# Index scores of a hybrid decoder block as 64-row products among MLA's first products, with turned blocks of x in places of their own

## What is computed

```python
h = rmsnorm(x, g[NORM_PRE_MIX])
(q_lat, kv_lat, k_rope, ..., idx_q, idx_k, idx_w, ...) = split_cols(h @ w_in[l])
# MLA: 8 heads of 128+64, from latents
q = rmsnorm(q_lat, q_norm) @ w_uq          # latents 384 wide
kv = rmsnorm(kv_lat, kv_norm) @ w_ukv      # latents 256 wide
# DSA's index scores: 8 heads of 64, one key shared by all heads
score = einsum('bth,bths->bts', iw, relu(einsum('bthd,bsd->bths', iq, ik)))
score = where(s <= t, score, -inf);  _, idx = top_k(score, 128)
```

## Time and profile before

| | us |
|---|---|
| median of 3 runs | 1501.98 (1501.86 to 1502.58) |
| the profiled execution | 1502.69 |
| its span in the profile | 1500.9 |
| PE busy | 1462.5 (97%) |
| DVE busy | 684.4 (46%) |
| ACT busy | 569.8 (38%) |
| mean granted PE clock | 0.997 |

### The profile page before, as it was taken

How to read it: one execution, slowest core, us unless ns; L and a number is a source line. 1 busy time by engine, 2 the same in 40 slices (tenths; PEclk the granted TensorE clock), 3 DMA queues, 4 the chain that set the end, 5 groups by cost and what they waited for, 6 DMA issues and landing times.

```text
span 1500.9 us, 17329 instructions
## 1 busy us (share of the span) xinstructions
PE 1462.5 (97%) x7180; PEld 1178.6 (79%) x7180; DVE 684.4 (46%) x1186; ACT 569.8 (38%) x920; POOL 99.7 (7%) x74
## 2 busy tenths in 40 slices
PE   6999999999999999999999999999999999999998
PEld 5957777887877788876776788897778888888886
DVE  3566565764333355444554344483355332222334
ACT  4444543214333243445345423454344342223321
POOL 1000000022220001000000001000000220011100
PEclk9999999999999999999999999999999999999999
DMA  5211132232311334440210333254121323233321
GB/s 178 79 38 46 43 112 78 91 104 79 99 56 57 93 113 156 148 145 15 70 57 3 125 117 136 85 173 137 56 85 57 112 84 113 84 99 99 95 102 56
DMA packets 118270, 137.87 MB, mean 92 GB/s; under 512 B 7043, under 2 KB 98432, under 8 KB 118192
## 3 DMA queue, kind: packets, MB, share of 16 engines
q1 hardware_dynamic: 115200, 126.17, 26.6%
q0 software_dynamic: 2704, 10.00, 1.9%
q10 hardware_dynamic: 288, 0.59, 0.1%
HBM read 134.61 MB, written 2.14 MB: 91 GB/s over the span
## 4 chain that ended last, share of the span: by engine, by line
PE 94%; ACT 2%; DVE 2%; issue 1%; DMA 0%; SPq 0%; DVEq 0%; ACTq 0%
PE dense L660 25%; PE dense L662 25%; PE dense L661 25%; PE score L773 3%; PE turned L790 3%; PE score L790 3%; PE turned L773 2%; PE turned L783 1%; PE score L763 1%; PE score L783 1%; DVE probs L1893 1%; ACT probsT L1268 1%; PE score L1166 1%; PE score L1152 0%; PE turned L1152 0%
## 5 line engine op out<-in xcount | busy, mean ns | idle before, releaser
L1739 DVE TENSOR_TENSOR weight_low<-raw,weight_high 128x2048 fp32r<-128x2048 f32 (+2 forms) x96 | 201.2, 2102 | 375.0 <-ACT weight_high L1268 374.9
L660 PE MATMUL dense<-hidden_high,weight_high 128*128 128x512 f32 (+1 forms) x840 | 327.0, 389 | 4.0 <-ACT vN L1268 2.5
L662 PE MATMUL dense<-hidden_high,weight_low 128*128 128x512 f32 (+1 forms) x840 | 320.7, 382 | 0.0
L661 PE MATMUL dense<-hidden_low,weight_high 128*128 128x512 f32 (+1 forms) x840 | 320.2, 381 | 0.0
L1268 ACT ACTIVATE weight_high<-raw 128x2048 fp32r<-128x2048 f32 (+4 forms) x156 | 220.8, 1440 | 257.5 <-PE dense L662 255.0
L660 PEld LDWEIGHTS dense<-hidden_high,weight_high 128*128 128x128 f32 x840 | 158.0, 188 | 34.2 <-ACT vN L1268 2.9
L662 PEld LDWEIGHTS dense<-hidden_high,weight_low 128*128 128x128 f32 x840 | 157.9, 188 | 31.0
L661 PEld LDWEIGHTS dense<-hidden_low,weight_high 128*128 128x128 f32 x840 | 158.1, 188 | 29.7 <-issue 0.7
L1734 DVE TENSOR_TENSOR weight_low<-raw,weight_high 128x1024 fp32r<-128x1024 f32 x58 | 74.9, 1334 | 67.5 <-ACT weight_high L1268 67.5
L660 PE MATMUL dense<-weight_high,up_high 128*128 128x512 f32 x256 | 99.6, 389 | 0.0
L661 PE MATMUL dense<-weight_low,up_high 128*128 128x512 f32 x256 | 99.6, 389 | 0.0
(11 more groups left out here) (311 smaller groups left out, 2326.9 us busy)
## 6 DMA issues: line engine op xcount, KB each, us to landing
raw<-in_w_in SPq DMA_DIRECT2D x34, 1024.0 KB, 5.3
raw<-in_mlp_w SPq DMA_DIRECT2D x32, 1024.0 KB, 5.3
raw<-in_w_branch SPq DMA_DIRECT2D x12, 1024.0 KB, 5.1
raw<-in_nsa_cmp_w SPq DMA_DIRECT2D x8, 1024.0 KB, 5.3
raw<-in_cross_wkv SPq DMA_DIRECT2D x8, 1024.0 KB, 5.6
raw<-in_w_in SPq DMA_DIRECT2D x9, 512.0 KB, 5.1
bias_strips<-bias_scratch POOLq DMA_DIRECT2D x8, 512.0 KB, 4.1
raw<-in_w_out SPq DMA_DIRECT2D x4, 1024.0 KB, 5.1
```

The source lines that it names most:

```text
L660: pe.matmul(out_ap, ah, bh, start=first, stop=False)
L661: pe.matmul(out_ap, ah, bl, start=False, stop=False)
L662: return pe.matmul(out_ap, al, bh, start=False, stop=last)
L1739: ins = V.tensor_tensor(dst, src, hi.bitcast(F32), ALU.subtract)
```

## The change

- **Start.** SP issues slab 0 right behind x and the six small loads behind it. The turned blocks 0 to 3 of x go to `W`, `SS`, `G[1]` and again `W` (`XB`), so that the first three wait for nothing but their scaling. Block 3 is turned in the middle of `("lat", 0)`, behind its first block's products. The small tables are turned after `("lat", 0)`, into `SS`. ACT copies half of slab 0 between the blocks of x. DVE makes the first half of slab 0's low part, POOL only the second. DVE copies the tables after the low part of slab 2.
- **Index scores.** One key tile holds the key twice, in rows 0 to 63 and 64 to 127. A product takes 64 rows of query and key; `index_pair` issues two of them, one on each half of the rows, for two heads. The products go through four places (`INDEX`), and product n waits for ACT's taking of n-4. Three pairs stand around the third turn of the latents; two stand in `m1`, three in `m2`, two in `m3`, two in `m4` of round 0. PE waits for the last taking after `m4`. ACT's ReLUs and DVE's sums are cut into pieces among the other steps: DVE does 16, then the rotation and a slab's low part, then 8.

```diff
-ikT = [at(f"index_k{i}", [P, T], 120 + 2 * i) for i in range(2)]
+ikT = at("index_k", [P, T], 120)
...
-product("setup", "V")
-for i in range(4):
-  product(("x", i), "V")
-for i in range(3):
+XB = [W, SS, G[1], W]
+for i in range(NT - 1):
+  part(None)
+  ready_at["x", i] = events[0]
+part(None)
+ready_at["x", NT - 1] = events[0]
+product(("lat", 0), "A", slab_at["lat", 0])
+part(None)
+ready_at["setup"] = events[0]
+for i in range(1, 3):
...
+INDEX = [S[0], S[1], PT, OT]
+INDEX_FIRST = 6
...
+hidden_split = sem("hidden_split")
+setup_taken = sem("setup_taken")
...
+  def load(s):
+      if s >= 2:
+          sp.wait_ge(low_ready, split_at[s - 2])
+      for src, view in slabs[s]:
+          sp.dma_start(view(raw[s % 2]), src).then_inc(loaded[s % 2], 16)
+  load(0)
...
-  def load(s):
-      if s >= 2:
-          sp.wait_ge(low_ready, split_at[s - 2])
-      for src, view in slabs[s]:
-          sp.dma_start(view(raw[s % 2]), src).then_inc(loaded[s % 2], 16)
-  for s in range(2):
-      load(s)
+  load(1)
...
-  g = product_at["setup"]
...
+  def turn_x(t):
+      pe.wait_ge(x_scaled, t + 1)
+      if t == NT - 1:
+          pe.wait_ge(hidden_split, 1)
+      for k in range(KD):
+          mm = pe.transpose(XB[t][:, k // 4, k % 4 * P:(k % 4 + 1) * P], xN[:, t, k * P:(k + 1) * P], ident[:, :])
+      mm.then_inc(product_ready, 1)
+  for t in range(NT - 1):
+      turn_x(t)
+  def hidden_tile(t):
+      if t == 1:
+          turn_x(NT - 1)
+      pe.wait_ge(hidden_split, t + 1)
+  g, s = product_at["lat", 0], slab_at["lat", 0]
+  n_mode(s, tokens_out(g), all_cols, KD, hT, wait_tile=hidden_tile).then_inc(product_ready, 1)
...
-  pe.transpose(G[0][:, 0, 0:61], gainRows[0:61, :], ident[0:61, 0:61])
-  pe.transpose(G[0][:, 0, 64:128], posRows[:, :], ident[0:64, 0:64])
-  pe.matmul(G[0][0:16, 1, :], tab[:, :], onehot[:, :], start=True, stop=True).then_inc(product_ready, 1)
-  for t in range(NT):
-      g = product_at["x", t]
-      free(g)
-      pe.wait_ge(x_scaled, t + 1)
-      for k in range(KD):
-          mm = pe.transpose(G[g % 2][:, k // 4, k % 4 * P:(k % 4 + 1) * P], xN[:, t, k * P:(k + 1) * P], ident[:, :])
-      mm.then_inc(product_ready, 1)
-  def hidden_tile(t):
-      pe.wait_ge(taken["V"], taken_count[product_at["x", t]])
-  for i in range(2):
-      g, s = product_at["lat", i], slab_at["lat", i]
-      free(g)
-      n_mode(s, tokens_out(g), all_cols, KD, hT, wait_tile=None if i else hidden_tile).then_inc(product_ready, 1)
+  pe.transpose(SS[:, 0, 0:61], gainRows[0:61, :], ident[0:61, 0:61])
+  pe.transpose(SS[:, 0, 64:128], posRows[:, :], ident[0:64, 0:64])
+  pe.matmul(SS[0:16, 1, :], tab[:, :], onehot[:, :], start=True, stop=True).then_inc(product_ready, 1)
+  g, s = product_at["lat", 1], slab_at["lat", 1]
+  n_mode(s, tokens_out(g), all_cols, KD, hT).then_inc(product_ready, 1)
...
-  pe.wait_ge(lat_scaled, NT)
-  for i in range(3):
+  def turn_latents(i):
...
+  pe.wait_ge(lat_scaled, NT)
+  for i in range(2):
+      turn_latents(i)
...
-  n = 0
-  for i in range(1, NT):
-      for h in range(8):
-          if n >= 2:
-              pe.wait_ge(index_taken, n - 1)
-          pe.matmul(S[n % 2][:, 0:(i + 1) * P], iqT[:, h // 2, i * P:(i + 1) * P],
-                    ikT[h % 2][:, 0:(i + 1) * P], start=True, stop=True).then_inc(index_ready, 1)
-          n += 1
-  pe.wait_ge(index_taken, INDEX_TILES)
+  pe.wait_ge(setup_taken, 1)
+  index_next = [0]
+  def index_pair():
+      for half in range(2):
+          n = index_next[0]
+          i, h = 1 + n // 8, n % 8
+          rows = slice(64 * half, 64 * half + 64)
+          if n >= 4:
+              pe.wait_ge(index_taken, n - 3)
+          pe.matmul(INDEX[n % 4][:, 0:(i + 1) * P], iqT[rows, h // 2, i * P:(i + 1) * P],
+                    ikT[rows, 0:(i + 1) * P], start=True, stop=True).then_inc(index_ready, 1)
+          index_next[0] += 1
+  for n in range(0, INDEX_FIRST, 2):
+      if n == 4:
+          turn_latents(2)
+      index_pair()
+  def index_chunk(first, count):
+      return lambda k: index_pair() if first <= k < first + count else None
...
-             2, (latH[:, 3:5, :], latL[:, 3:5, :])).then_inc(product_ready, 1)
+             2, (latH[:, 3:5, :], latL[:, 3:5, :]), wait_tile=None if p else index_chunk(0, 2)).then_inc(product_ready, 1)
...
-      t_mode(s, two(g), [uq_cols(0), uq_cols(128)], 3, lat).then_inc(product_ready, 1)
+      t_mode(s, two(g), [uq_cols(0), uq_cols(128)], 3, lat, None if p else index_chunk(1, 2)).then_inc(product_ready, 1)
...
-      t_mode(s, two(g)[0:1], [uq_cols(256)], 3, lat).then_inc(product_ready, 1)
+      t_mode(s, two(g)[0:1], [uq_cols(256)], 3, lat, None if p else index_chunk(0, 3)).then_inc(product_ready, 1)
...
-             2, (latH[:, 3:5, :], latL[:, 3:5, :]), ahead(begin, 2) if p else None).then_inc(product_ready, 1)
+             2, (latH[:, 3:5, :], latL[:, 3:5, :]), ahead(begin, 2) if p else index_chunk(0, 2)).then_inc(product_ready, 1)
...
+      if p == 0:
+          pe.wait_ge(index_taken, INDEX_TILES)
...
-      copy(hTH[:, :, t * P:(t + 1) * P], bank(("x", t))[:, :, :].rearrange("p b (k c) -> p (b k) c", c=P)).then_inc(hidden_high, 1)
+      copy(hTH[:, :, t * P:(t + 1) * P], XB[t][:, :, :].rearrange("p b (k c) -> p (b k) c", c=P)).then_inc(hidden_high, 1)
...
-  x_high(0)
-  high(0)
-  for t in range(1, NT):
+  for k, (dst, src) in enumerate(half_pieces(0, wh[0], raw[0])):
+      x_high(k)
+      act.wait_ge(loaded[0], landed[0])
+      copy(dst, src).then_inc(high_ready, 1)
+  for t in range(2, NT):
...
-  n = 0
-  for i in range(1, NT):
-      for h in range(8):
+  def index_relu(first, last):
+      for n in range(first, last):
+          cols = (2 + n // 8) * P
...
-          nc.scalar.activation(relu[:, n % 2, 0:(i + 1) * P], S[n % 2][:, 0:(i + 1) * P], ACT.Relu).then_inc(index_taken, 1)
-          n += 1
+          nc.scalar.activation(relu[:, n % 2, 0:cols], INDEX[n % 4][:, 0:cols], ACT.Relu).then_inc(index_taken, 1)
+  index_relu(0, INDEX_FIRST + 4)
...
+      if p == 0:
+          index_relu(INDEX_FIRST + 4, INDEX_FIRST + 10)
...
+      if p == 0:
+          index_relu(INDEX_FIRST + 10, INDEX_FIRST + 14)
...
+      else:
+          index_relu(INDEX_FIRST + 14, INDEX_TILES)
...
-      V.tensor_tensor(hTL[:, :, c], bank(("x", t))[:, :, :].rearrange("p b (k c) -> p (b k) c", c=P),
-                      hTH[:, :, c].bitcast(F32), ALU.subtract).then_inc(taken["V"], 1)
+      V.tensor_tensor(hTL[:, :, c], XB[t][:, :, :].rearrange("p b (k c) -> p (b k) c", c=P),
+                      hTH[:, :, c].bitcast(F32), ALU.subtract).then_inc(hidden_split, 1)
...
-  ready("setup")
-  b0 = bank("setup")
-  V.tensor_copy(gains, b0[:, 0, 0:61])
-  V.tensor_copy(posT, b0[:, 0, 64:128])
-  V.tensor_copy(biasRow[:, P:], b0[0:16, 1, :]).then_inc(taken["V"], 1)
+  x_low(0)
+  dve.wait_ge(high_ready, 1)
+  c = slice(0, KD // 2)
+  V.tensor_tensor(wl[0][:, c, :], raw[0][:, c, :], wh[0][:, c, :].bitcast(F32), ALU.subtract).then_inc(low_ready, 1)
...
-  for t in range(NT):
+  for t in range(1, NT):
...
+  ready("setup")
+  V.tensor_copy(gains, SS[:, 0, 0:61])
+  V.tensor_copy(posT, SS[:, 0, 64:128])
+  V.tensor_copy(biasRow[:, P:], SS[0:16, 1, :]).then_inc(setup_taken, 1)
...
-      dve.wait_ge(index_zeroed, 2)
-      V.tensor_copy(ikT[0][0:64, :], b[64:128, 0, :])
-      V.tensor_copy(ikT[1][64:128, :], b[64:128, 0, :]).then_inc(taken["V"], 1)
+      V.tensor_copy(ikT[0:64, :], b[64:128, 0, :])
+      V.tensor_copy(ikT[64:128, :], b[64:128, 0, :]).then_inc(taken["V"], 1)
...
-  n = 0
...
-  for i in range(1, NT):
-      for h in range(8):
+  def index_add(first, last):
+      for n in range(first, last):
+          i, h = 1 + n // 8, n % 8
...
-          n += 1
-      dve.wait_ge(index_added, n)
-      d = iscore[:, TRI[i] - P + i * P:TRI[i] - P + (i + 1) * P]
-      link(V.tensor_tensor(d, d, strip0[:, T - P:], ALU.add))
+          if h == 7:
+              dve.wait_ge(index_added, n + 1)
+              d = iscore[:, TRI[i] - P + i * P:TRI[i] - P + (i + 1) * P]
+              link(V.tensor_tensor(d, d, strip0[:, T - P:], ALU.add))
+  index_add(0, INDEX_FIRST + 10)
...
+      if p == 0:
+          index_add(INDEX_FIRST + 10, INDEX_TILES)
...
-  for t in ikT:
-      Q.memset(t[:, :], 0.0).then_inc(index_zeroed, 1)
...
-  for k in range(2):
-      pool.wait_ge(high_ready, k + 1)
-      c = slice(k * KD // 2, (k + 1) * KD // 2)
-      Q.tensor_tensor(wl[0][:, c, :], raw[0][:, c, :], wh[0][:, c, :].bitcast(F32), ALU.subtract).then_inc(low_ready, 1)
+  pool.wait_ge(low_ready, 1)
+  pool.wait_ge(high_ready, 2)
+  c = slice(KD // 2, KD)
+  Q.tensor_tensor(wl[0][:, c, :], raw[0][:, c, :], wh[0][:, c, :].bitcast(F32), ALU.subtract).then_inc(low_ready, 1)
...
-  pool.wait_ge(taken["V"], taken_count[product_at["setup"]])
+  pool.wait_ge(setup_taken, 1)
...
```

(1 more changed line is left out.)

## The result

The changed kernel takes 1492.78 us (median of four runs, 1492.01 to 1493.62); the kernel before, beside it, 1502.23 (1501.86 to 1502.58). The ratio is 0.9937, 95% interval 0.992 to 0.9954: 9.45 us, or 0.6%, faster, inside the range of 1491.0 to 1499.0 and two microseconds more than the forecast gain of 7.5. The profiled executions took 1492.01 (span 1490.2) and 1502.69 (span 1500.9).

What follows compares the result with a forecast made beforehand. PE, 94% of the chain of waits, was taken as the bound. The start's 3.0 us and the index stage's 4.5 make 7.5, so 1495.2 us profiled or 1494.5 as a median; range 1491.0 to 1499.0.

Steps and rivals of the forecast that it cites:

- What bounds the kernel: PE is 94% of the chain of waits; what is gained by the first score at 120.05 should reach the end.
- the prediction's signs of being wrong: Pair over 2 us, PE waiting in `m4`, half clock beyond 24 us, or first-score-to-end distance changing over 1 us.
- Start: Start of PE's list: `("lat", 0)` near 15.8 instead of 22.54; gain 1.2 to 4.2 us, 3.0 taken.
- the 12 instructions and 8 turns: PE's work behind slab 0's second half, before the other 72 instructions: priced mostly at half clock, 2.2 and 1.6 us.
- Places of the pairs: Index stage: three pairs go early around the latents' third turn, so `m1` begins at 91.1 instead of 107.61.
- A pair at three quarters: Index stage: a pair's products overlap partly, only the two outer instructions alone; nine pairs cost 9.6 us.
- rival 1: Index stage: pairs overlap fully, nine cost 6.4 us; total gain 10.0 us, 1492.0; chance 0.15.
- Switch: Index stage: PE going from 128 rows to 64 and back costs 0.33 us a pair, 3.0 us for nine.
- Rival 3: Index stage: PE drains at every change of rows, also between a pair's heads; slower, 1506.7 us; chance 0.04.
- No wait added: Index stage: DVE's last ReLU is done at 114.6, 0.9 us before PE asks, so PE waits no longer.
- Rival 2: Index stage: 64-row products do not overlap, nine pairs cost 12.8 us; total gain 3.8 us, 1498.2; chance 0.22.
- Rival 4: Rounds 1 to 3: a slab or DVE is late, only 2 us of 7.5 arrive, 1500; chance 0.05.

Runs made afterwards that it cites:

- e3: Changed kernel with index products of 128 rows again (two keys padded with zeros), same places of order and PSUM: 1495.85 us, ratio 0.9957.
- e5: Changed kernel with both halves of slab 0's low part on DVE, none on POOL: 1492.09 us, ratio 0.9933.
- e8: Changed kernel with both halves of slab 0's low part on DVE and the nine pairs in five groups: 1491.74 us, ratio 0.9926.
- e1_start: Changed kernel with the index stage of before, so the start's part of the change alone: 1499.88 us, ratio 0.9983.
- e0_again: The changed kernel run again with no edit: 1493.67 us, ratio 0.9948.
- e4_same_rows: Changed kernel with both products of a pair on rows 0 to 63: 1499.99 us, ratio 0.9991.
- e7_grouped: Changed kernel with the nine pairs in five groups, DVE doing 14 sums instead of 16 ahead of the rotation: 1492.78 us, ratio 0.9936.
- e6_order: Changed kernel with pairs one place earlier in `m1`, one pair instead of two in `m4`, 18 sums ahead of the rotation: 1493.64 us, ratio 0.9942.
- e9_both_late: Against e8: only four products ahead of `m1`, ten pairs in six groups behind, 16 sums ahead of the rotation: 1492.93 us, ratio 0.9937.
- e2_index: Changed kernel with the start of before, so the index stage's part of the change alone: 1495.86 us, ratio 0.9959.

## Why the prediction was right, by its steps

- **What bounds the kernel: held.** What was gained by the first score reached the end. From there to the end of the span took 1380.85 before and 1379.30 after, which is 1.55 apart, over the 1 us that I had named as the limit. One of the prediction's signs of being wrong has shown, but its cause is no mechanism of the change: of the twelve profiles, the four with a half-clock stretch between 654 and 669 us (before, e3, e5, e8) lie at 1380.7 to 1380.9, the other eight at 1379.2 to 1379.5.
- **Start, 3.0 forecast: 2.84 in the profiles, 2.5 in the medians of e1_start.** `("lat", 0)` near 15.8 was 15.87, slab 0 at 13.5 as taken. The terms written down add up to 32.3 for `("lat", 1)`, a gain of 2.5; the 3.0 was chosen above that sum, and 31.84 was measured. Behind slab 0 two terms were wrong and partly cancelled, so that the total came out well is in part luck. POOL's half was priced at 2.34 and took 2.86, so the second half came at 19.48 instead of 18.7. Against that the 12 instructions and 8 turns took 1.54 and 0.80 instead of 2.2 and 1.6, for the clock stayed full in this execution. Where it fell, with the same 1.9 us of idle ahead (e0_again, e1_start, e3_padded), `("lat", 2)` stood at 45.0 to 45.3 and the gain was 1.0 to 1.3, at the lower end of my 1.2 to 4.2 or just under it.
- **Places of the pairs: held.** `m1` began 6.6 us after the turn of the latents, against 6.9 in the forecast.
- **A pair at three quarters, 9.6 us for nine: this step failed.** They cost 6.4, rival 1's value. The reason I gave, that PE starts in order and a product is two instructions, was no obstacle: the first instructions of both heads start 6 ns apart, then the second ones, 7 ns apart. This is what the Trainium skill, TensorE: Matmul & The Clock Gate, Part 3, says of different row groups (about 4 ns apart); the trace agrees that they run at once, with 6 to 7 ns, for float32 products of 64 rows. I had given that 0.15. The forecast of the total held all the same, because the 3.2 us too much here were partly made up by switches and waits that I had too low.
- **Switch, 0.33 each: 0.41**, within 0.2 to 0.5. e3_padded and e4_same_rows show it alone, e7_grouped that it is paid per change of rows. Nine make 3.7 instead of 3.0. The rule that changing the tiling mode drains TensorE (the Trainium skill, TensorEngine Tiling (Array Packing), Key Properties) is borne out as far as a late start after each change of the number of rows goes, and none in e3_padded, where it doesn't change; of the 0.41, 0.19 to 0.20 are the two late starts and 0.21 the wider first distance after each. Rival 3, a drain between the two heads as well, is excluded by the 6 ns.
- **No wait added: this failed too**, and it was a sign of being wrong that I had named. PE waited 0.40 in the second pair of `m4` and 0.36 before the first score. The timeline of DVE shows why:

```profile
93.32 0.42 DVE L1910 TENSOR_SCALAR index_score<-index_relu,small 128x384 f32<-128x384 f32 x1 [1.08 <-ACT index_relu L1395]
...
95.75 1.34 DVE L1913 SCALAR_TENSOR_TENSOR index_score<-index_relu,small,index_score 128x384 f32<-128x384 f32 x2 [1.29 <-ACT index_relu L1395]
...
100.85 0.69 DVE L1849 TENSOR_TENSOR q_rope<-dense,cosT 128x512 f32<-128x512 f32 x1
...
108.46 3.31 DVE L1913 SCALAR_TENSOR_TENSOR index_score<-index_relu,small,index_score 128x512 f32<-128x512 f32 x4 [0.42 <-ACT index_relu L1395]
```

DVE had 3.1 us of gaps ahead of the rotation (1.08, 1.29, 0.32, 0.40), where ACT's ReLUs had to wait for PE's next pair (ACT's own idle times before them are 1.51, 0.79 and 0.87) and once stood behind ACT's copy of `m1` (94.31 to 95.23). Its 16 sums ended at 100.82, so it began the rotation at 100.85. Its operand was there 1.35 us sooner: `m2`'s last instruction, at 99.10, ended at 99.50. From the rotation's start, 4.15 us of rotation and slab and eight sums end just behind PE's list (111.77 against 110.54). I read this as PE and DVE both being close to the limit; e6_order and e9_both_late gained nothing, which fits, but no run takes DVE's work away to show it.

The stage adds up: forecast 31.3 (115.5 less 84.24); 0.3 less to `m1`, 3.2 less for the pairs, 0.7 more for switches, 0.8 more for waits give 29.3, and 29.51 was measured. Some sums of the prediction don't come out of their own terms, none of them in the forecast: `("lat", 1)` with full clock is 31.0, not 30.6 (30.7 with slab 0 at 13.2); the forecast's own range is 1497.0 to 1492.3 with nine switches, not 1497.3 to 1492; rival 1 has PE at 112.3, not 112.7, where DVE's 113.1 decides anyway.

**Rival 2**, no overlap, is excluded by the pair's 1.06 us; e4_same_rows is that case, with 1.91. **Rival 4**, gain taken back later, did not occur.

## What to carry to other kernels

Two half-height products on different halves of TensorE's rows, with their own PSUM banks, took PE as long as one (0.85 us for 512 columns); but each excursion from full rows and back cost 0.41 us, so they should be issued in groups, and here the switches ate two thirds of the overlap. First place the small products among other work, where the consumer would otherwise make PE wait, and give them more places to land in: both together brought 4.3 of the 6.3 us. Then ask what the consumer's own chain allows: here, with PE waiting 0.4 us for the last ReLU, moving products about (e6_order, e9_both_late) brought nothing more.

## What the runs showed of the hardware that I had not expected

- Two float32 products of two MATMULs each, in two halves of the rows, interleave: starts 99.424, 99.430, 99.957, 99.964. On the same half (e4_same_rows) they follow one another: 102.849, 103.383, 103.812, 104.241.
- A stretch at half clock comes and goes between executions of one kernel: at 20.0 to 23.4 us in e0_again and not in the first profile, which cost 1.56 us, half of the start's gain. Between 654 and 669 us four of the twelve profiles have one and eight have none, 1.2 to 1.7 us apart in what follows the first score. PE stands idle ahead of it (663 to 664 us before), but equally so in the change (654 to 655 us), where none follows; what decides is not shown. Such stretches explain part of the scatter of the run times.
- In e2_index the windows show the granted clock full throughout, yet the dense instructions of 256 columns stand 0.21 us apart until 25.8 us and not 0.12. The same holds for the turns of x in the change: 8 of them take 1.71 us from 11.97 to 13.68, where the column also reads 1.00, and 0.80 from 21.02. So at the start of a trace the distances of MATMULs tell the rate, and the column of the clock doesn't.
- POOL's subtraction of half a slab took 2.86 us while DVE had no pause beside it, and 2.34 in the earlier trace rows, where DVE paused for 1.6 of the 4.7 us. That DVE is the reason was not tested.
